# One VectorE step order for a two-layer attention block: weight splits, modulation sums and a turn moved to other places

## The chip, the cores and the metric

The kernel runs on one core of a Trainium2 chip. The metric is the device time of one execution in microseconds (us). It is taken as the median of several runs. A core has a matmul engine (TensorE, PE in the profile), a vector engine (VectorE, DVE), a scalar engine (ScalarE, ACT), GpSimd (POOL), and a queue that issues transfers (SyncE, SP). Each takes its instructions strictly in the order in which they are written, and they wait for one another on semaphores.

## The reference

The program computes two blocks. The change touches the first one only: two layers on 256 tokens of 1024 features, each with its own modulation.

```
cs = jax.nn.silu(c)
for l in range(DEPTH):                       # DEPTH = 2
    mod = cs @ w_ada[l] + b_ada[l]
    shift, scale, gate = mod[:, None, :D], mod[:, None, D:2 * D], mod[:, None, 2 * D:]
    h = rmsnorm(x, g_pre[l]) * (1.0 + scale) + shift
    y = hybrid_mixer(h, w_in[l], w_out[l], pe_k[l], pe_v[l], w_ck1[l], w_ck2[l], w_cv1[l], w_cv2[l])
    x = x + gate * rmsnorm(y, g_post[l])
...
    u = h @ w_in                             # hybrid_mixer: all projections from one product
...
    logits = jnp.concatenate([s_sel.reshape(MOBA_HEADS, Q_CHUNK, KM * MOBA_BLOCK), s_own], axis=-1)
    p = jax.nn.softmax(logits, axis=-1).astype(v_own.dtype)
...
    y = jnp.concatenate([o_m * jax.nn.silu(zm), o_n * jax.nn.silu(zn)], axis=-1)
    return y @ w_out
```

The mixer holds three kinds of attention (moba, selected and windowed) and one over compressed keys. The second block (neighbourhood attention, feed-forward, latent attention, eight experts) takes most of the time and is unchanged.

## The kernel before

**Two kinds of steps on one stream.** All weights come from memory as pieces of 128x2048 numbers (1 MB). SP issues them into a ring of six buffers `raw` (L681), in the order of the list `STEPS`. A piece is one of two kinds.

- `("w", n)`: a weight of a projection. A float32 product is made as three products of a high and a low part (`mm3`, L833 to L835), so the piece is split: ScalarE copies the rounded high part (`hi_to`, w_hi, L1625), then VectorE subtracts it (`raw_to`, w_lo, L2211). The splits live in a ring of three, so split n waits until TensorE has used split n-3. Below, w9 is the split of piece 9.
- `("ada", j, half)`: half of the modulation's part j. VectorE multiplies its four columns of 512 by the conditioning and adds them up in `acc` (four instructions, L2227 and L2229, in `raw_to` too). TensorE then sums over partitions with a product with ones (`ada`, L903 and L908), in bank 3, and ScalarE copies the result out (`ada_out`). Below, a3.1 is the second half of part 3. Parts 0 to 3 are shift and scale, 4 and 5 the gate.

A `raw` buffer is free when VectorE has done the step. Phase `pre` holds the first layer's parts 0 to 3. Phase `lay0` is the first layer and holds its parts 4 and 5 and parts 0 to 5 of the second layer. Phase `lay1` is the second layer and holds parts 0 to 5 of the next block's modulation.

**The start.** VectorE makes the eight halves of `pre`, with the norm of x (`normed`) after four of them. After the last, PE sums part 3, ScalarE copies it, VectorE makes scale and shift (`make_ab`), and then h, the normalised and modulated input, is made in four blocks: ScalarE and VectorE scale them, ScalarE makes the high parts (`h_hi`), and VectorE the low ones (`norm`, `lo(b)`). The first projection needs half of h and split 0 for its first half, and the rest of h and split 1 for its second. ScalarE copies out parts 1 to 3 and then makes the high parts of splits 0 to 2 (`hi_to(SPL)`), ahead of `h_hi`.

**The ticks.** After three projections comes a loop of 25 ticks (`LAY_TICKS`) over 24 pairs of heads. In tick i TensorE makes the scores of pair i+1, one or more pieces of the projections that are left (`fill`, table `LAY_FILL`), the turn (transpose) of the probabilities of pair i, further pieces, and the product of the values of pair i-1 (`values`; of a group's first pair in the next tick, and only when `finish` has emptied the output bank). VectorE makes the logits of pair i+1 (L2530), the finishing of a group of four pairs (`finish`), single operations of the compressed branch (`cmp_u` in tick 0 to `cmp_y` in tick 7), and at the tick's end the steps of `STEPS` up to a mark that `lay_steps_before` gives. ScalarE makes the exponentials of pair i+1 (L1880), copies the turned probabilities (L1894), empties the banks of a finished projection (`slot`), copies a modulation part (`ada_out`), and last makes the high part of the next split. A split's low part on VectorE so waits for a high part that comes last in ScalarE's tick, after the exponentials of that same tick's logits.

**The sums in the ticks.** `LAY_ADA` says in which tick TensorE sums which part: {1: 0, 4: 1, 9: 2, 10: 3, 12: 4, 15: 5}, always after the tick's scores and ahead of its projection pieces. In tick 1 it waits ahead of that for `cmp_u` and in tick 4 for `clogits`, since bank 3 is shared with the compressed branch. In tick 18 TensorE turns a part of y for the output projection (`turn_y`, L1014), which waits for `finish(3)`.

The order of VectorE's steps by tick of the first layer, before:

```
before the ticks  w0 w1 w2 | a4.0 w3 a4.1 w4 (of this layer) | a5.0 w5 a5.1 w6 | a0.0 w7 a0.1 w8 (of the next)
tick 2: a1.0 a1.1 w9     tick 4: a2.0 w10     tick 6: a2.1 a3.0 w11     tick 8: a3.1 w12
tick 9: a4.0 w13         tick 11: a4.1 a5.0 w14     tick 13: a5.1 w15
tick 15: w16     tick 16: w17     tick 18: w18     tick 22: w19
```

## Time and profile before

| | us |
|---|---|
| median of 3 runs (lowest to highest) | 1642.2 (1639.86 to 1644.54) |
| the profiled execution, device time | 1639.46 |
| its span in the trace | 1637.6 |
| PE busy, share of the span | 1412.2 (86%) |
| DVE busy, share of the span | 1215.8 (74%) |
| ACT busy, share of the span | 860.8 (53%) |
| first layer, from the start to its last product | 245.8 |
| second layer, to its last product | 453.9 |

The profiled execution stands 2.7 us under the median, and its span 1.9 us under its own device time. The two layers are the first 28% of the span. Times in the rows are in us from the span's start. A number in square brackets at a row's end is how long the engine was idle ahead of it, and who released it.

### The profile page before, as it was taken

How to read it: one execution, taken by the hardware profiler on the slowest of the kernel's cores; microseconds unless marked ns; L12 is line 12 of the kernel's file. 1: busy time of each engine (PE TensorE's matmuls, PEld its weight loads, DVE VectorE, ACT ScalarE, POOL GpSimd, SP SyncE). 2: the span in 40 equal slices, each digit the busy share in tenths (PEclk: the TensorE clock that was granted, in tenths of full speed). 3: DMA queues.
4: the chain of work that ended last, by engine and by line, in shares of the span. 5: the costliest groups of instructions: out<-in, count | busy, mean ns of one | idle time of the engine just before them, and what ended most of it. 6: DMA issues, size and time to landing. Idle time of an engine off the chain costs nothing.

```text
span 1637.6 us, 21240 instructions
## 1 busy us (share of the span) xinstructions
PE 1412.2 (86%) x7628; PEld 1185.4 (72%) x7628; DVE 1215.8 (74%) x1484; ACT 860.8 (53%) x1210; POOL 65.3 (4%) x82
## 2 busy tenths in 40 slices
PE   2799987899879996899985896999999999999992
PEld 2778777787668776898974875877777777777772
DVE  6777646776575747788857545789889888899895
ACT  2333534445443543343324635577677777777772
POOL 1000000000010000000001004000000000000001
PEclk8899998989988997999987996999999999999996
DMA  9765514545256623677763214899999999899782
GB/s 399 274 235 181 211 72 172 227 180 206 77 215 236 242 96 127 262 289 272 290 236 122 104 52 146 302 345 357 351 345 360 345 348 373 338 358 362 286 365 90
DMA packets 61537, 403.08 MB, mean 246 GB/s; under 512 B 6534, under 2 KB 9734, under 8 KB 15116
## 3 DMA queue, kind: packets, MB, share of 16 engines
q1 hardware_dynamic: 52416, 379.45, 61.2%
q10 hardware_dynamic: 7020, 15.17, 2.6%
q0 software_dynamic: 2016, 7.34, 1.2%
q8 instruction: 52, 0.85, 0.2%
q14 instruction: 33, 0.27, 0.0%
HBM read 393.01 MB, written 8.91 MB: 245 GB/s over the span
## 4 chain that ended last, share of the span: by engine, by line
PE 49%; DVE 32%; ACT 10%; issue 5%; DMA 2%; POOL 1%; ACTq 0%; DVEq 0%; SPq 0%; POOLq 0%
DVE w_lo L2211 18%; PE PS L833 13%; PE PS L835 12%; PE PS L834 12%; ACT w_hi L1625 4%; DVE acc L2229 4%; ACT xg L1720 2%; PE PS L903 1%; PE PS L986 1%; PE PS L1006 1%; DVE a_lo L2378 1%; DVE hb L2387 1%; DVE hb L2389 1%; DVE h_lo L2344 1%; PE PS L995 1%
## 5 line engine op out<-in xcount | busy, mean ns | idle before, releaser
L2211 DVE TENSOR_TENSOR w_lo<-raw,w_hi 128x2048 fp32r<-128x2048 f32 x287 | 659.4, 2298 | 156.4 <-ACT w_hi L1625 133.7
L1625 ACT ACTIVATE w_hi<-raw 128x2048 fp32r<-128x2048 f32 x287 | 547.7, 1919 | 243.3 <-PE PS L835 230.3
L833 PE MATMUL PS<-w_hi,h_hi 128*128 128x512 f32 (+2 forms) x812 | 335.3, 413 | 25.0 <-DVE h_lo L2654 7.3
L835 PE MATMUL PS<-w_hi,h_lo 128*128 128x512 f32 (+2 forms) x812 | 318.8, 393 | 0.0
L834 PE MATMUL PS<-w_lo,h_hi 128*128 128x512 f32 (+2 forms) x812 | 318.1, 392 | 0.0
L833 PE MATMUL PS<-h_hi,w_hi 128*128 128x256 f32 x776 | 235.2, 303 | 43.4 <-DVE w_lo L2211 19.4
L834 PE MATMUL PS<-h_lo,w_hi 128*128 128x256 f32 x776 | 227.4, 293 | 0.0
L835 PE MATMUL PS<-h_hi,w_lo 128*128 128x256 f32 x776 | 227.2, 293 | 0.0
L833 PEld LDWEIGHTS PS<-w_hi,h_hi 128*128 128x128 f32 x812 | 155.8, 192 | 72.8 <-DVE w_lo L2211 14.9
L2229 DVE SCALAR_TENSOR_TENSOR acc<-raw,cs,acc 128x512 f32<-128x512 f32 x252 | 189.5, 752 | 9.0
L833 PEld LDWEIGHTS PS<-h_hi,w_hi 128*128 128x128 f32 x776 | 156.9, 202 | 48.4 <-DVE w_lo L2211 19.6
L835 PEld LDWEIGHTS PS<-w_hi,h_lo 128*128 128x128 f32 x812 | 155.4, 191 | 32.8
L834 PEld LDWEIGHTS PS<-w_lo,h_hi 128*128 128x128 f32 x812 | 155.8, 192 | 28.6 <-issue 2.2
L834 PEld LDWEIGHTS PS<-h_lo,w_hi 128*128 128x128 f32 x776 | 156.8, 202 | 2.4 <-issue 1.7
L835 PEld LDWEIGHTS PS<-h_hi,w_lo 128*128 128x128 f32 x776 | 156.5, 202 | 0.0
L833 PE MATMUL PS<-w_hi,a_hi 128*128 128x512 f32 x340 | 140.2, 412 | 17.1 <-DVE a_lo L2378 11.1
L835 PE MATMUL PS<-w_hi,a_lo 128*128 128x512 f32 x340 | 134.5, 396 | 0.0
L834 PE MATMUL PS<-w_lo,a_hi 128*128 128x512 f32 x340 | 133.7, 393 | 0.0
L1880 ACT ACTIVATE lgp<-lgp,st 128x128 f32<-128x128 f32 (+1 forms) x96 | 42.9, 448 | 121.1 <-DVE st L2530 121.1
L833 PEld LDWEIGHTS PS<-w_hi,a_hi 128*128 128x128 f32 x340 | 64.6, 190 | 37.3 <-DVE w_lo L2211 22.9
L835 PEld LDWEIGHTS PS<-w_hi,a_lo 128*128 128x128 f32 x340 | 64.4, 189 | 14.7
L834 PEld LDWEIGHTS PS<-w_lo,a_hi 128*128 128x128 f32 x340 | 64.6, 190 | 11.9
(310 smaller groups left out, 1394.5 us busy)
## 6 DMA issues: line engine op xcount, KB each, us to landing
raw<-in_ws SPq DMA_DIRECT2D x359, 1024.0 KB, 5.6
y_rows<-ysb ACTq DMA_DIRECT2D x10, 512.0 KB, 7.6
rp<-in_rp ACTq DMA_DIRECT2D x8, 384.0 KB, 4.7
ckb<-in_ck ACTq DMA_DIRECT2D x2, 1024.0 KB, 4.8
y_rows<-ones ACTq DMA_DIRECT2D x3, 512.0 KB, 8.5
x<-in_x SPq DMA_DIRECT2D x1, 1024.0 KB, 13.4
gpost<-in_gpost ACTq DMA_DIRECT2D x2, 512.0 KB, 6.0
x_rows<-xn_f ACTq DMA_DIRECT2D x2, 512.0 KB, 3.9
```

Source lines behind the costliest of these rows:

```text
L833: t.matmul(out, lhs[0], rhs[0], start=start, stop=False, skip_group_check=True)
L834: t.matmul(out, lhs[0], rhs[1], start=False, stop=False, skip_group_check=True)
L835: return t.matmul(out, lhs[1], rhs[0], start=False, stop=stop, skip_group_check=True)
L903: last = t.matmul(PS[:, 3, c:c + 1], a[:, c * P:(c + 1) * P], ones[:, 0:1], start=True, stop=True)
L986: t.matmul(PS[:, PS_S[i % 2], 0:2 * u["nk"]].rearrange("p (a k) -> p a k", a=2), u["q"], u["k"], start=True, stop=True).then_inc(*e.inc("s ...
L995: last = t.transpose(PS[:, PS_PT, c * P:(c + 1) * P], lgp[:, i % 3, c * P:(c + 1) * P], ident)
L1006: last = t.matmul(PS[:, PS_O, h * HD:(h + 1) * HD], ptp[:, i % 2, (a * n + c) * P:(a * n + c + 1) * P], u["v"][a][c], start=c == 0, stop=c ...
L1625: a.activation(wh[:, SPL_AT[e.phase][i], :], raw[:, r, :], ACT.Copy).then_inc(*e.inc("hi"))
L1720: ins = a.activation(xg[:, kt, :], PS[:, 6 + kt // 4, (kt % 4) * P:(kt % 4 + 1) * P], ACT.Identity, scale=ab[:, 0, kt:kt + 1], bias=ab[:, ...
L1880: a.activation(part, part, ACT.Exp, bias=mn(c), scale=-1.0, accum_out=sm(c)).then_inc(*e.inc("probs"))
L2211: v.tensor_tensor(wl[:, s, :], raw[:, r, :], wh[:, s, :].bitcast(F32), ALU.subtract).then_inc(*e.inc("raw_used"))
L2229: ins = v.scalar_tensor_tensor(out=dst, in0=w, scalar=c[:, kt:kt + 1], in1=dst, op0=ALU.mult, op1=ALU.add)
```

## The change

It changes the order of work in the first block and no computation.

- **Start.** ScalarE makes the high part of split 0 between the copies of parts 1 and 2, and that of split 1 between those of parts 2 and 3. Split 2 comes after `h_hi`. VectorE does five halves ahead of `normed` in place of four, and the low part of split 0 ahead of `make_ab`.
- **Steps.** `layer_steps` gives a new order of the stream, w7 and w8 ahead of the sums, and VectorE goes through it by a table, `LAY_STEP`, one or two steps a tick up to tick 14. The second half of part 0 moves from ahead of the ticks into tick 0.
- **Sums.** On TensorE part 3 moves from tick 10 to 11 and part 4 from tick 12 to 13. Parts 0 and 1 (ticks 1 and 4) move to the end of their tick, with the waits for `cmp_u` and `clogits`, and so does the turn of y in tick 18.
- **Last split.** w19 moves from tick 22 to tick 23 on VectorE.

```
before the ticks  w0 | w1 w2 a4.0 w3 a4.1 w4 (of this layer) | a5.0 w5 a5.1 w6 w7 w8 | a0.0 (of the next)
tick 0: a0.1     tick 1: a1.0     tick 2: w9 a1.1     tick 4: w10     tick 5: a2.0     tick 6: w11     tick 7: a2.1
tick 8: w12 a3.0     tick 9: w13     tick 10: a3.1     tick 11: w14 a4.0     tick 12: a4.1 a5.0
tick 13: w15     tick 14: a5.1     tick 15: w16     tick 16: w17     tick 18: w18     tick 23: w19
```

The diff, cut to its core:

```
-LAY_ADA = {1: 0, 4: 1, 9: 2, 10: 3, 12: 4, 15: 5}
+LAY_ADA = {1: 0, 4: 1, 9: 2, 11: 3, 13: 4, 15: 5}
+
+LAY_STEP = [("ada", 0, 1), ("ada", 1, 0), ("ada", 1, 1), ("ada", 1, 1), ("w", 10), ("ada", 2, 0), ("w", 11), ("ada", 2, 1),
...
@@ tensor, in the ticks
-                    if i == 1:
-                        pe.wait_ge(*e.at("cmp_u", 1))
-                    if i == 4:
-                        pe.wait_ge(*e.at("clogits", 1))
-                    if i in LAY_ADA:
+                    if i in LAY_ADA and i > 4:
                         ada(unit + LAY_ADA[i])
-                    if i == 18:
-                        pe.wait_ge(*e.at("y", 2))
-                        bank_free(1)
-                        turn_y(1, 1, 1)
...
                         values(i - 1)
+                    if i in (1, 4):
+
+                        pe.wait_ge(*e.at("cmp_u" if i == 1 else "clogits", 1))
+                        ada(unit + LAY_ADA[i])
+                    if i == 18:
+                        pe.wait_ge(*e.at("y", 2))
+                        bank_free(1)
+                        turn_y(1, 1, 1)
@@ scalar, start
-            for j in range(1, 4):
-                ada_out(j, 1)
+            ada_out(1, 1)
             e.resume("lay0")
-            hi_to(SPL)
+            hi_to(1)
+            e.resume("pre")
+            ada_out(2, 1)
+            e.resume("lay0")
+            hi_to(2)
+            e.resume("pre")
+            ada_out(3, 1)
+            e.resume("lay0")
@@ vector
-            raw_to(4)
+            raw_to(5)
...
-                    split_to(1)
+                split_to(1)
...
-                split_to(9)
+                raw_to(step_of("ada", 0, 0))
...
-                    split_to(lay_steps_before(i) + SPL)
+                    if i < len(LAY_STEP):
+                        raw_to(step_of(*LAY_STEP[i]))
+                    else:
+                        split_to(min(lay_steps_before(i) + SPL, 19 if i < 23 else 20))
```

ScalarE at the start. L1680 copies a modulation part out in the kernel before (L1683 in the one after), L1625 (L1628) makes a high part, L1654 and L1658 (L1657 and L1661) are blocks of h. Before:

```order
L1680 ACTIVATE modc<-PS 128x4 x3
L1625 ACTIVATE w_hi<-raw 128x2048 x3
L1654 ACTIVATE hb<-PS,ab 128x256 x2
L1658 ACTIVATE h_hi<-hb 128x512 x2
L1651 DMA ckb<-in_ck 128x2048
```

After:

```order
L1683 ACTIVATE modc<-PS 128x4
L1628 ACTIVATE w_hi<-raw 128x2048
L1683 ACTIVATE modc<-PS 128x4
L1628 ACTIVATE w_hi<-raw 128x2048
L1683 ACTIVATE modc<-PS 128x4
L1657 ACTIVATE hb<-PS,ab 128x256 x2
L1661 ACTIVATE h_hi<-hb 128x512 x2
```

Two of the three high parts stand between the copies, and nothing stands between the last copy and the first block of h.

VectorE at the start, from the norm of x on (L2251 before, L2260 after). Before:

```order
L2251 TENSOR_SCALAR xn_l<-x,st 128x1024 x2
L2227 TENSOR_SCALAR acc<-raw,cs 128x512
L2229 SCALAR_TENSOR_TENSOR acc<-raw,cs,acc 128x512 x7
L2227 TENSOR_SCALAR acc<-raw,cs 128x512
L2229 SCALAR_TENSOR_TENSOR acc<-raw,cs,acc 128x512 x7
L2288 TENSOR_TENSOR modc<-modc,par 128x16
L2290 SCALAR_TENSOR_TENSOR ab<-modc,par 128x8
L2294 COPY ab<-modc 128x8
L2270 TENSOR_SCALAR hb<-PS,ab 128x256 x2
L2262 TENSOR_TENSOR h_lo<-hb,h_hi 128x512
L2270 TENSOR_SCALAR hb<-PS,ab 128x256 x2
L2262 TENSOR_TENSOR h_lo<-hb,h_hi 128x512 x3
```

After:

```order
L2260 TENSOR_SCALAR xn_l<-x,st 128x1024 x2
L2238 SCALAR_TENSOR_TENSOR acc<-raw,cs,acc 128x512 x4
L2236 TENSOR_SCALAR acc<-raw,cs 128x512
L2238 SCALAR_TENSOR_TENSOR acc<-raw,cs,acc 128x512 x7
L2220 TENSOR_TENSOR w_lo<-raw,w_hi 128x2048
L2297 TENSOR_TENSOR modc<-modc,par 128x16
L2299 SCALAR_TENSOR_TENSOR ab<-modc,par 128x8
L2303 COPY ab<-modc 128x8
L2279 TENSOR_SCALAR hb<-PS,ab 128x256 x2
L2271 TENSOR_TENSOR h_lo<-hb,h_hi 128x512
L2279 TENSOR_SCALAR hb<-PS,ab 128x256 x2
L2271 TENSOR_TENSOR h_lo<-hb,h_hi 128x512 x3
```

One half of a sum has gone ahead of the norm, and the low part of split 0 ahead of `make_ab`.

VectorE in ticks 6 and 7 of the first layer. The first y is the end of `cmp_y(0)` in tick 6, and lgp and st are logits. Before:

```order
L2609 TENSOR_TENSOR y<-y,tmpo 128x512
L2229 SCALAR_TENSOR_TENSOR acc<-raw,cs,acc 128x512 x4
L2227 TENSOR_SCALAR acc<-raw,cs 128x512
L2229 SCALAR_TENSOR_TENSOR acc<-raw,cs,acc 128x512 x3
L2211 TENSOR_TENSOR w_lo<-raw,w_hi 128x2048
L2530 ISA lgp,st<-lc,PS 128x128
```

After:

```order
L2622 TENSOR_TENSOR y<-y,tmpo 128x512
L2220 TENSOR_TENSOR w_lo<-raw,w_hi 128x2048
L2543 ISA lgp,st<-lc,PS 128x128
L2543 ISA st 128x1
L2543 ISA lgp,st<-lc,PS 128x128
L2543 ISA st 128x1
L2612 RECIPROCAL st<-st 128x8
L2613 TENSOR_TENSOR st<-st,vsw 128x8
L2617 TENSOR_TENSOR y<-PS,st 128x512
L2238 SCALAR_TENSOR_TENSOR acc<-raw,cs,acc 128x512 x4
```

Tick 6 has lost two halves of sums and keeps w11 alone, which now has nothing of the stream ahead of it. One of the halves stands in tick 7, the other in tick 8.

TensorE at the change from tick 10 to 11 of the first layer. L986 (L989) are scores, L903 (L906) the sum of part 3, and L1006 (L1009) values. Before, from the scores of tick 10 on:

```order
L835 MATMUL PS<-h_hi,w_lo 128x256
L986 MATMUL PS<-kswz,qn 128x256
L903 MATMUL PS<-ones,acc 128x1 x4
L1006 MATMUL PS<-vsw,ptp 128x64 x2
L833 MATMUL PS<-h_hi,w_hi 128x256
```

After, from the values at the end of tick 10 on:

```order
L838 MATMUL PS<-h_hi,w_lo 128x256
L1009 MATMUL PS<-vsw,ptp 128x64 x2
L989 MATMUL PS<-kswz,qn 128x512
L906 MATMUL PS<-ones,acc 128x1 x4
L836 MATMUL PS<-w_hi,h_hi 128x512
```

The sum of part 3 now stands behind the scores of tick 11, ahead of that tick's projection pieces.

## Rows read from the trace of the kernel before

**Rows 1.** The page's chain that ended last, by engine, as shares of the span.

```profile
PE 49%; DVE 32%; ACT 10%; issue 5%; DMA 2%; POOL 1%; ACTq 0%; DVEq 0%; SPq 0%; POOLq 0%
```

**Rows 2.** Stretches, both layers' ticks: length, busy PE, PEld, DVE, ACT, POOL, clock, DMA.

```profile
94.53:210.43 115.90, 107.14 (x614) 87.00 (x612) 84.64 (x180) 53.28 (x135) 0.00 (x0) 0.94 0.50 187
301.32:416.97 115.65, 103.98 (x609) 86.14 (x609) 83.37 (x179) 53.30 (x135) 0.00 (x0) 0.96 0.50 187
```

**Rows 3.** Timeline of PE at the start: start, duration, instruction, idle before.

```profile
33.79 1.87 PE L903 MATMUL PS<-ones,acc 128*128 128x1 f32 x8 [4.98 <-DVE acc L2229]
51.70 0.58 PE L833 MATMUL PS<-h_hi,w_hi 128*128 128x256 f32 x1 [16.05 <-DVE w_lo L2211]
```

**Rows 4.** Timeline of ACT at the start.

```profile
35.76 5.50 ACT L1625 ACTIVATE w_hi<-raw 128x2048 fp32r<-128x2048 f32 x3
41.16 1.01 ACT L1654 ACTIVATE hb<-PS,ab 128x256 f32<-128x256 f32 x2
```

**Rows 5.** Timeline of DVE at the start.

```profile
35.97 0.18 DVE L2288 TENSOR_TENSOR modc<-modc,par 128x16 f32<-128x16 f32 x1 [2.23 <-ACT modc L1680]
...
49.36 6.95 DVE L2211 TENSOR_TENSOR w_lo<-raw,w_hi 128x2048 fp32r<-128x2048 f32 x3
```

**Rows 6.** Line L681, the issues of pieces 0 and 1, with time to landing.

```profile
L681 SPq DMA_DIRECT2D raw<-in_ws x1: 328/328/328, 15.6 to 15.6; - x1
...
DMA to landing us min/median/max: 15.8/15.8/15.8
...
L681 SPq DMA_DIRECT2D raw<-in_ws x1: 327/327/327, 18.7 to 18.7; - x1
...
DMA to landing us min/median/max: 15.1/15.1/15.1
```

**Rows 7.** DVE groups by line, first layer's ticks: count, busy, mean ns, idle before.

```profile
L2229 DVE SCALAR_TENSOR_TENSOR acc<-raw,cs,acc 128x512 f32<-128x512 f32 x35 | 26.3, 752 | 1.2
L2211 DVE TENSOR_TENSOR w_lo<-raw,w_hi 128x2048 fp32r<-128x2048 f32 x11 | 25.2, 2292 | 18.3 <-ACT w_hi L1625 18.1
```

**Rows 8.** Timeline of DVE in the ticks of the first layer.

```profile
94.53 0.29 DVE L2530 CUSTOM_DVE_ANT_0 lgp<-lc,PS 128x128 f32<-128x128 f32 x1 [0.22 <-DVE vsw L2677]
...
196.81 0.29 DVE L2530 CUSTOM_DVE_ANT_0 lgp<-lc,PS 128x128 f32<-128x128 f32 x1 [0.23 <-DVE w_lo L2211]
...
200.19 2.29 DVE L2211 TENSOR_TENSOR w_lo<-raw,w_hi 128x2048 fp32r<-128x2048 f32 x1 [2.76 <-ACT w_hi L1625]
```

**Rows 9.** Timeline of ACT in tick 15 of the first layer.

```profile
191.29 0.60 ACT L1894 ACTIVATE ptp<-PS 128x512 f32<-128x512 f32 x1 [0.25 <-PE PS L995]
191.79 0.59 ACT L1682 ACTIVATE gate<-PS 128x512 f32<-128x512 f32 x1
192.26 1.92 ACT L1625 ACTIVATE w_hi<-raw 128x2048 fp32r<-128x2048 f32 x1
```

**Rows 10.** Timeline of PE in the ticks of the first layer.

```profile
120.69 0.49 PE L903 MATMUL PS<-ones,acc 128*128 128x1 f32 x3 [2.55 <-DVE ce L2579]
...
149.02 0.58 PE L833 MATMUL PS<-h_hi,w_hi 128*128 128x256 f32 x1 [2.92 <-ACT qm L1829]
...
154.87 0.95 PE L903 MATMUL PS<-ones,acc 128*128 128x1 f32 x8
```

**Rows 11.** Stretches around two PE waits, with the granted clock (last but two).

```profile
145.20:148.60 3.40, 0.91 (x6) 0.50 (x5) 2.81 (x9) 1.72 (x7) 0.00 (x0) 1.00 0.90 354
148.60:152.00 3.40, 2.98 (x14) 2.98 (x15) 3.22 (x8) 1.85 (x8) 0.00 (x0) 0.50 0.65 270
...
206.60:210.00 3.40, 3.40 (x13) 2.13 (x11) 1.66 (x7) 2.05 (x7) 0.00 (x0) 0.51 0.02 10
```

**Rows 12.** Timelines of DVE and PE near the end of the first layer.

```profile
229.30 2.29 DVE L2211 TENSOR_TENSOR w_lo<-raw,w_hi 128x2048 fp32r<-128x2048 f32 x1 [4.61 <-ACT w_hi L1625]
...
232.37 0.50 PE L833 MATMUL PS<-w_hi,h_hi 128*128 128x512 f32 x1 [1.14 <-DVE h_lo L2654]
```

**Rows 13.** Timeline of ACT before the ticks of the second layer.

```profile
292.92 1.90 ACT L1625 ACTIVATE w_hi<-raw 128x2048 fp32r<-128x2048 f32 x1
```

More of the change, by code:

```diff
@@ L53 @@
 LAY_FILL = [(1, 2) if i % 4 == 3 and i < 16 else (1, 1) for i in range(18)] + [(0, 0)] * (LAY_TICKS - 18)
-LAY_ADA = {1: 0, 4: 1, 9: 2, 10: 3, 12: 4, 15: 5}
+LAY_ADA = {1: 0, 4: 1, 9: 2, 11: 3, 13: 4, 15: 5}
+LAY_STEP = [("ada", 0, 1), ("ada", 1, 0), ("ada", 1, 1), ("ada", 1, 1), ("w", 10), ("ada", 2, 0), ("w", 11), ("ada", 2, 1),
+            ("ada", 3, 0), ("w", 13), ("ada", 3, 1), ("ada", 4, 0), ("ada", 5, 0), ("w", 15), ("ada", 5, 1)]
 LAY_OUT = {19: 2, 20: 2, 21: 2, 22: 2}
@@ L98, in layer_steps @@
 def layer_steps(gates):
-    place = [(6, 0, 0), (7, 0, 1), (8, 1, 0), (8, 1, 1), (9, 2, 0), (10, 2, 1), (10, 3, 0), (11, 3, 1),
-             (12, 4, 0), (13, 4, 1), (13, 5, 0), (14, 5, 1)]
+    place = [(8, 0, 0), (8, 0, 1), (8, 1, 0), (9, 1, 1), (10, 2, 0), (11, 2, 1), (12, 3, 0), (13, 3, 1),
+             (14, 4, 0), (14, 4, 1), (14, 5, 0), (15, 5, 1)]
     out = []
@@ L2519, in layer, with step_of @@
                     gate_post()
+                def step_of(kind, n, half=None):
+                    step = ("w", n) if kind == "w" else ("ada", n + 6 * (l == 0), half)
+                    return STEPS[e.phase].index(step) + 1
                 def logits(i):
```

## The prediction

> **What bounds the kernel now.** I read the chain that ended last first, to see which engines hold the end. PE has half of it, and VectorE and ScalarE another 42% [rows 1], so no engine is bound by itself and hand-overs between the three count. Then I took the stretch from a layer's first logits to its output projection. It is 115.90 us in the first layer and 115.65 in the second, while PE is busy for 107.1 and 104.0 of it [rows 2]. PE could save at most 9 to 12 us a layer there. The timelines show where PE stands still. Before the first projection it waits 16.05 us, for the low part of split 0 [rows 3]. In the ticks it waits 2.55 us for the compressed branch's logits, ahead of the sum of part 1, and 2.92 us for a bank that ScalarE empties late [rows 10]. At the end of the layer there is a wait of 1.14 us [rows 12].
>
> **The start.** At 33.79 PE sums part 3, ScalarE copies it, and three high parts follow at 35.76, 5.50 us long, ahead of the first block of h at 41.16 [rows 3, 4]. Piece 0 lands at 15.6 + 15.8 = 31.4 us and piece 1 at 18.7 + 15.1 = 33.8 [rows 6]. So ScalarE can make the first high part at 31.4 to 33.3. Only then does it copy part 2 (33.5). PE needs bank 3 from that copy for part 3: 33.5 in place of 33.79. The second high part runs at 33.8 to 35.7, the copy of part 3 ends at 35.9, and `make_ab` starts at 36.0, as before at 35.97 [rows 5]. Nothing is gained up to here, and the norm that VectorE makes one half later is hidden. The first block of h then starts at 36.6 in place of 41.16: 4.6 us. PE's first product needed, after half of h at 45.4, two more low parts of h and the low part of split 0 at 49.36 to 51.7 [rows 5]. That low part is now there first, so PE starts at about 40.9 in place of 51.70: **10.8 us**. The later splits follow. The low part of split 1 ends at 47.2 and PE asks for it at 49.3. After that each split costs VectorE 2.29 and half a sum about 2.9 [rows 7], under PE's 5.8 a split. Piece 4 is issued when split 0 is done, 16 us sooner. Ahead of the ticks a0.1 (3.1 us) is gone, but w8 now waits for a high part that had been hidden behind it. Of the 3.1 us some 0.5 are left: the first logits start at **83.2 in place of 94.53, 11.3 us earlier**. The second layer has no such start. There its high part 8 runs from 292.92 [rows 13], its low part ends at 297.2 and a0.0 at 300.1, so the first logits come 0.9 us earlier.
>
> **The ticks.** Durations: a low part 2.32 with its gap, a first half of a sum 2.86, a second half 3.14 (4 x 0.752 and gaps) [rows 7]. A pair of logits takes 0.86 or 1.1. The hand-over decides. From the start of a pair's logits it takes two exponentials, the copy of the turned probabilities and a high part until the low part can start: 200.19 - 196.81 = 3.38 us [rows 8], and 3.97 for the wide pairs. Before, in all seven such ticks up to tick 13, VectorE made one or two halves of sums first and hid all or part of that time. Now the low part comes first, and the half behind it. I walked VectorE through the new table from 83.2, each low part at the later of VectorE's own end and ScalarE's high part:
>
> - tick 0 with a0.1 ends at 90.0, tick 1 with a1.0 at 95.2.
> - tick 2: logits 95.4, w9 at 98.8, VectorE idle 2.75. Tick 3: the compressed logits end at 111.5.
> - tick 4: w10 at 115.9 (idle 2.2). PE sums part 1 at 111.6 at once.
> - tick 6: w11 at 128.1 (1.1). Tick 8: w12 at 139.2 (2.7). Tick 9: w13 at 148.1 (0.9). Tick 10: a3.1 ends at 154.5.
>
> Up to there PE is ahead. At tick 8 it is at 133.8 where it was at 149.02 [rows 10], 15 us earlier. But then it runs into the moved sums. The sum of part 3 stands ahead of tick 11's pieces and turn, and PE reaches it at 152 and waits until 154.5. Behind it stand the turn of pair 11, the copy on ScalarE, the high part 14 and the low part 14: 0.8 + 1.5 + 0.5 + 0.4 + 2.0 later, at 159.8, and VectorE idles 4 us from 155.6. The same ring comes twice more. a4.1 ends at 169.3 and PE, there at 166.4, starts the sum of part 4. w15 starts at 176.9, a5.1 ends at 183.5, PE is there at 180.7. After that sum (2.0), a piece (1.5) and the turn, ScalarE copies, copies the gate and starts the high part 16 0.97 after its copy [rows 9]. VectorE starts w16 at 190.6 and w17 at 196.55, which ends at 198.85. Before, w17 ended at 202.5 [rows 8]. From the first logits on that is 115.65 against 107.95 us, so **the ticks cost 7.7 us more in the first layer**, and by the same walk 7.95 in the second, whose stretch was 0.25 us shorter before [rows 2]. Of the 7.7, 3.1 are a0.1, which moved in, and the rest low parts that wait in the open. PE's 2.55, 2.92 and later waits do vanish. They are replaced by four of 2.5 to 4 us in ticks 10, 11, 13 and 15, the first of them ahead of the values of pair 8, for VectorE's `finish(1)`.
>
> **The end of a layer.** The low part 19 holds VectorE until 231.6, after a wait of 4.61, and the low part of y behind it lets PE start at 232.37 [rows 12]. With w19 behind it, that low part starts 1.05 us earlier, and w19 is still ready 0.6 us before PE needs it: **1.05 us less in each layer**. The turn of y in tick 18 moves nothing. What PE needs next is a low part in tick 19 that the logits of tick 18 lead to.
>
> **The clock.** After PE stood for 2.9 us the next 3.4 us had the granted clock at 0.50, the 1.2 GHz level, and so had a stretch after the wait at 203 [rows 11]. At half the clock PE's work takes up to twice as long. The new waits in ticks 11, 13 and 15 are as long, and what runs behind them (sum, piece, turn) is on the ring. Each such stretch can cost up to 1.6 us: 0 to 4.8 a layer. I take 2.3, half, since part of a stretch falls on work that has room: **4.6 us**, bounds 0 and 9.6.
>
> The Trainium skill, "TensorE: Matmul & The Clock Gate", section "Why this matters for your kernels", sets the limit for a harmless gap in PE's work somewhat above these lengths. By it the term would be 0. This trace does not agree, since it shows the drop behind 2.92 us.
>
> **The sum.** -11.3 (start) + 7.7 - 1.05 (first layer) - 0.9 + 7.95 - 1.05 (second) + 4.6 (clock) = +6.0 us, rounded. On the profiled execution's 1639.5 that is 1645.5. It stood 2.7 under the median, so the median goes from 1642.2 to **1648.2**.
>
> **The rivals.**
>
> 1. The ring doesn't cost clock. Everything else as above: +1.4, 1643.6. For it: a stretch at the low clock that starts late falls on pieces ahead of the next wait, and then only shortens that wait. Chance 0.30.
> 2. **Faster.** The ticks keep their length, because the sums find their halves ready and ScalarE's high parts come soon enough: -11.3 - 0.9 - 2.1 = -14.3, 1628. For it: PE is 15 us ahead at tick 8 and has no wait of its own left. Against it: VectorE's own work from tick 8 to 15 with its open waits is longer than PE's. It decides whether a3.1 ends before PE stands at the sum of part 3, for which VectorE must be 2.5 us sooner. Chance 0.17.
> 3. The start brings little: ScalarE is in order, so if pieces 0 and 1 land late, the copies of parts 2 and 3 and so h wait for them. Each us of delay costs one, all of it gone would be 1648.2 + 11 = 1659. The landings in the rows speak against it, with 0.1 us of room. Chance 0.06, and as much again for what I don't see.
>
> My forecast has 0.41. The range goes from 1634 (rival 1 with the ticks 10 us cheaper in all by my reading of hand-overs) to 1657 (all of the clock term and 4 more). A change of 0.3%, 4.9 us, is about what a measurement of this kernel can tell from none. Slower by more than that is most of the forecast and of rival 3 and a little of rival 1: 0.46. Within it: 0.34. Faster: 0.20.
>
> **What would show it.** In the trace after: the first product at 41 and the first logits near 83 (the start). VectorE idle ahead of each low part in ticks 2, 8 and 11, by 2.7, 2.7 and 4 us. PE waiting for acc at the sums of ticks 11, 13 and 15, some 3 us each, and no wait for the bank in tick 8. From first logits to output projection about 123.6 us and more, against 115.9. The granted clock at 0.50 behind the new waits. I am wrong if that stretch stays under 118 in both layers, or if the first product starts after 45.

## The result and the profile after

The changed kernel takes 1649.8 us (median of 6 runs, 1648.5 to 1654.2) against 1642.4 us (median of 6, 1639.9 to 1644.5). The ratio is 1.0054, 95% interval 1.0038 to 1.0069. It is **7.5 us slower**, where 6.0 was forecast.

The profiled execution of after was the longest of its six, 1654.2 us with a span of 1652.4, and the one of before was short for its kernel (1639.5, span 1637.6). So the two traces stand 14.8 us apart, twice the medians. What follows reads places and sizes from the traces, and the worth of an edit from the medians.

The stretches of both layers' ticks, from the first logits to the output projection, answer to [rows 2], in the same columns:

```profile
84.14:214.54 130.40, 112.73 (x616) 89.73 (x615) 87.70 (x184) 53.30 (x135) 0.00 (x0) 0.91 0.47 172
305.28:433.14 127.86, 111.06 (x609) 88.78 (x608) 86.42 (x183) 53.15 (x135) 0.00 (x0) 0.91 0.49 176
```

With the boundaries on PE (the transposes that open the second layer start at 254.57 before and 259.31 after, those of the phase behind it at 462.69 and 477.81), the difference of the traces lies here:

| stretch | before | after | difference |
|---|---|---|---|
| start to first logits | 94.53 | 84.14 | -10.4 |
| ticks, first layer | 115.90 | 130.40 | +14.5 |
| end of the first layer | 44.14 | 44.77 | +0.6 |
| second layer to its logits | 46.75 | 45.97 | -0.8 |
| ticks, second layer | 115.65 | 127.86 | +12.2 |
| end of the second layer | 45.72 | 44.67 | -1.05 |
| all behind the layers | 1174.9 | 1174.6 | -0.3 |

The start first. The timeline of PE there (start, duration, instruction, idle before), against [rows 3]:

```profile
33.74 1.84 PE L906 MATMUL PS<-ones,acc 128*128 128x1 f32 x8 [5.72 <-ACT modc L1683]
41.42 0.55 PE L836 MATMUL PS<-h_hi,w_hi 128*128 128x256 f32 x1 [5.84 <-DVE h_lo L2271]
```

PE's wait ahead of the first product has fallen from 16.05 us to 5.84. It ends with h, since the low part of split 0 had been ready since 35.9. The other wait, ahead of the sum of part 3, was there before too (4.98 us, for VectorE). It is now 5.72, for ScalarE's copy of part 2, and the sum starts at nearly the same time (33.74, was 33.79).

In the ticks, VectorE's low parts wait. The timeline of VectorE in the first layer, ticks 2, 8, 11, 13, 15 and 16:

```profile
99.73 2.29 DVE L2220 TENSOR_TENSOR w_lo<-raw,w_hi 128x2048 fp32r<-128x2048 f32 x1 [2.75 <-ACT w_hi L1628]
...
140.30 2.29 DVE L2220 TENSOR_TENSOR w_lo<-raw,w_hi 128x2048 fp32r<-128x2048 f32 x1 [3.16 <-ACT w_hi L1628]
...
162.01 2.29 DVE L2220 TENSOR_TENSOR w_lo<-raw,w_hi 128x2048 fp32r<-128x2048 f32 x1 [5.46 <-ACT w_hi L1628]
...
182.32 2.29 DVE L2220 TENSOR_TENSOR w_lo<-raw,w_hi 128x2048 fp32r<-128x2048 f32 x1 [4.18 <-ACT w_hi L1628]
...
198.17 2.29 DVE L2220 TENSOR_TENSOR w_lo<-raw,w_hi 128x2048 fp32r<-128x2048 f32 x1 [8.43 <-ACT w_hi L1628]
...
204.30 2.29 DVE L2220 TENSOR_TENSOR w_lo<-raw,w_hi 128x2048 fp32r<-128x2048 f32 x1 [2.99 <-ACT w_hi L1628]
```

All low parts of this stretch together (line L2220: what VectorE sat idle for, us, times; the same question to before gave 12.4 us, 4 times):

```profile
  ACT w_hi L1628: 30.3, 9
```

And PE waits for VectorE's halves of sums, `acc` in the table of waits of PE for the same stretch (who waited for whom: us in total, times, longest; the line with `h_lo` is the wait that ends the stretch):

```profile
PE PS L911 <- DVE acc L2238: 4.5, 2, 3.1
PE PS L836 <- DVE h_lo L2667: 2.9, 1, 2.9
PE PS L906 <- DVE acc L2238: 2.8, 1, 2.8
```

The place where both meet is tick 11. PE reaches the sum of part 3 too early and stands for 2.78 us. The turn of pair 11 follows only at 158.99, on it ScalarE's copy at 159.66, its high part at 159.99 and VectorE's low part at 162.01:

```profile
155.49 1.05 PE L906 MATMUL PS<-ones,acc 128*128 128x1 f32 x8 [2.78 <-DVE acc L2238]
158.99 0.63 PE L998 MATMUL PS<-par,lgp 128*128 128x128 f32 x2
...
171.51 2.08 PE L911 MATMUL PS<-acc,ones 128*128 128x512 f32 x2 [3.11 <-DVE acc L2238]
173.52 2.07 PE L913 MATMUL PS<-brow,ones 1*128 1x512 f32 x2
175.52 0.80 PE L836 MATMUL PS<-w_hi,h_hi 128*128 128x512 f32 x1
...
178.25 1.05 PE L998 MATMUL PS<-par,lgp 128*128 128x128 f32 x4
```

```profile
159.66 0.38 ACT L1903 ACTIVATE ptp<-PS 128x256 f32<-128x256 f32 x1 [2.44 <-PE PS L998]
159.94 0.17 ACT L1683 ACTIVATE modc<-PS 128x4 f32<-128x4 f32 x1
159.99 1.92 ACT L1628 ACTIVATE w_hi<-raw 128x2048 fp32r<-128x2048 f32 x1
```

The sum of part 5 waits 1.39 us. At all three sums the granted clock falls to its lower level: from 156.5 to 159.9 behind the first, and at the other two as here (columns: window, length, busy PE, clock, DMA share, GB/s; compare [rows 11]):

```profile
166.80:170.20 3.40, 1.60 (x8) 1.00 0.99 361
170.20:180.40 10.20, 8.89 (x18) 0.50 0.68 255
180.40:190.60 10.20, 8.81 (x44) 1.00 0.34 113
190.60:197.40 6.80, 6.80 (x18) 0.51 0.34 142
```

In the ticks the clock stood at 1.2 GHz for 23.8 us in the first layer, where it had been 13.6 before, and for 24.0 in the second, where it had been 10.2.

What that did to the work is seen at the sum of part 4. In the lines above, the sum and the piece behind it take 4.01 and 2.73 us. In the kernel before, at 2.4 GHz, the same two took 2.00 and 1.52:

```profile
171.00 1.02 PE L908 MATMUL PS<-acc,ones 128*128 128x512 f32 x2
...
173.00 0.50 PE L833 MATMUL PS<-w_hi,h_hi 128*128 128x512 f32 x1
...
174.52 0.60 PE L995 MATMUL PS<-par,lgp 128*128 128x128 f32 x4
```

### The profile page after: what moved, and what is told of

Same layout as the page of the kernel before. It is cut to its first block, busy times and chain, and to the rows that moved or that the text cites. A ratio compares the mean times of both kernels' runs of the same rounds, so it can differ in the third digit from the quotient of the medians.

```text
span 1652.4 us, 21240 instructions
## 1 busy us (share of the span) xinstructions
PE 1425.1 (86%) x7628; PEld 1191.9 (72%) x7628; DVE 1216.2 (74%) x1484; ACT 861.0 (52%) x1210; POOL 65.5 (4%) x82
## 4 chain that ended last, share of the span: by engine, by line
PE 48%; DVE 33%; ACT 10%; issue 5%; DMA 3%; POOL 1%; ACTq 0%; DVEq 0%; SPq 0%; POOLq 0%
DVE w_lo L2220 17%; PE PS L836 13%; PE PS L838 12%; PE PS L837 12%; DVE acc L2238 5%; ACT w_hi L1628 4%; DMA raw<-in_ws 2%; ACT xg L1723 2%; DVE a_lo L2387 1%; DVE hb L2396 1%; DVE hb L2398 1%; DVE h_lo L2353 1%; PE PS L913 1%; PE PS L1009 1%; PE PS L911 1%
## 5 line engine op out<-in xcount | busy, mean ns | idle before, releaser
L2220 DVE TENSOR_TENSOR w_lo<-raw,w_hi 128x2048 fp32r<-128x2048 f32 x287 | 659.6, 2298 | 183.7 <-ACT w_hi L1628 161.3
L1628 ACT ACTIVATE w_hi<-raw 128x2048 fp32r<-128x2048 f32 x287 | 547.8, 1918 | 246.2 <-PE PS L838 222.2
L836 PE MATMUL PS<-w_hi,h_hi 128*128 128x512 f32 (+2 forms) x812 | 340.2, 419 | 26.7 <-DVE h_lo L2667 9.1
L837 PE MATMUL PS<-w_lo,h_hi 128*128 128x512 f32 (+2 forms) x812 | 321.9, 396 | 0.0
L836 PEld LDWEIGHTS PS<-w_hi,h_hi 128*128 128x128 f32 x812 | 158.6, 195 | 75.9 <-DVE w_lo L2220 14.8
L836 PE MATMUL PS<-w_hi,a_hi 128*128 128x512 f32 x340 | 140.3, 413 | 17.2 <-DVE a_lo L2387 11.2
L838 PEld LDWEIGHTS PS<-w_hi,a_lo 128*128 128x128 f32 x340 | 64.4, 190 | 14.7
L837 PEld LDWEIGHTS PS<-w_lo,a_hi 128*128 128x128 f32 x340 | 64.6, 190 | 11.8
```

The source lines that it names most:

```text
L836: t.matmul(out, lhs[0], rhs[0], start=start, stop=False, skip_group_check=True)
L837: t.matmul(out, lhs[0], rhs[1], start=False, stop=False, skip_group_check=True)
L838: return t.matmul(out, lhs[1], rhs[0], start=False, stop=stop, skip_group_check=True)
L1628: a.activation(wh[:, SPL_AT[e.phase][i], :], raw[:, r, :], ACT.Copy).then_inc(*e.inc("hi"))
L2220: v.tensor_tensor(wl[:, s, :], raw[:, r, :], wh[:, s, :].bitcast(F32), ALU.subtract).then_inc(*e.inc("raw_used"))
```

## Theory and rivals

The theory is the prediction's: the start gives some 11 us, and the new order of steps takes more than that back, through low parts of VectorE that wait in the open and through a **ring**: half of a sum on VectorE, the sum on PE, the turn behind it, ScalarE's copy and high part, VectorE's low part, and only then the next half. Rivals: the loss comes from the sums and the turn of y at a tick's end; from the clock behind PE's waits and not from the order; or the open low parts alone do it and no ring is closed. All ratios below are against the kernel before, timed on the same chip beside each experiment (1641.6, 1642.0 and 1642.1 us in the three groups), with the 95% interval.

## Experiments: the parts apart

**The start alone**, on the kernel before (in the first layer also `split_to(1)` ahead of `make_ab`):

```diff
-            for j in range(1, 4):
-                ada_out(j, 1)
...
-            hi_to(SPL)
+            ada_out(1, 1)
...
+            hi_to(1)
...
+            ada_out(2, 1)
...
+            hi_to(2)
...
+            ada_out(3, 1)
...
-            raw_to(4)
+            raw_to(5)
```

> The kernel before with the start of the change alone: the first high parts between the copies of parts 1, 2 and 3, raw_to(5), and the low part of split 0 ahead of make_ab in the first layer. If the start is worth what the sum says, first product at 41 and first logits 10.4 to 11.3 us earlier than 94.53 and nothing given back in the unchanged ticks: 1642.4 - 11 = 1631. Rival, the gain is lost again because VectorE has the same steps to do before PE needs them: 1638 to 1642, with new waits of PE in the ticks.

Measured: 1629.8 us, ratio 0.9927 (0.9908 to 0.9946), 11.8 us less. First product 41.29, first logits 84.58, ticks 114.9 and 115.7 us long, as before. The start is worth what the sum said, and the old order of steps gives nothing back.

**The new order of steps alone**, on the kernel before:

```diff
-    place = [(6, 0, 0), (7, 0, 1), ...
+    place = [(8, 0, 0), (8, 0, 1), ...
-LAY_ADA = {1: 0, 4: 1, 9: 2, 10: 3, 12: 4, 15: 5}
+LAY_ADA = {1: 0, 4: 1, 9: 2, 11: 3, 13: 4, 15: 5}
...
-                    split_to(lay_steps_before(i) + SPL)
+                    if i < len(LAY_STEP):
+                        raw_to(step_of(*LAY_STEP[i]))
+                    else:
+                        split_to(lay_steps_before(i) + SPL)
```

> The kernel before with the new order of steps alone (place, LAY_STEP, the sums of parts 3 and 4 one tick later, the step a0.0 as the last ahead of the ticks); sums 0 and 1, the turn of y and w19 stand where they stood, and the start is the old one. If the order of steps costs 7.7 and 7.95 us in the ticks, less 0.9, and the clock 4.6: 1642.4 + 19.4 = 1662. If the clock costs nothing: 1657. Rival, the loss of the change sits in the turn and the sums at a tick's end and not in the steps: 1645 or less.

Measured: 1674.6 us, ratio 1.0198 (1.0182 to 1.0215), **33 us more**. The loss is in the order of steps, and larger than forecast. The ticks are 135.8 and 132.9 us. Part of it is a pairing that the full change does not have: with the sums of parts 0 and 1 at a tick's start, PE stands ahead of them too, 3.10 us in tick 1 (3.36 in the second layer, where the trace names the half of part 0) and 3.98 in tick 4, for the compressed logits, where it had been 2.55 [rows 10].

**The ends alone**: sums 0 and 1 and the turn of y at a tick's end, and w19 in tick 23, on the kernel before:

```diff
-                    if i in LAY_ADA:
+                    if i in LAY_ADA and i > 4:
                         ada(unit + LAY_ADA[i])
...
                         values(i - 1)
+                    if i in (1, 4):
...
+                        ada(unit + LAY_ADA[i])
+                    if i == 18:
...
+                        turn_y(1, 1, 1)
```

> The kernel before with the sums of parts 0 and 1 and the turn of y in tick 18 at the tick's end on PE, and w19 in tick 23 in place of 22, nothing else. If PE's waits in tick 4 (2.55 and 3.0 us) are hidden by VectorE's chain, only w19 counts, 1.05 us a layer: 1642.4 - 2.1 = 1640.3. Rival, these waits are on the path and go: 5 us more, 1635.

Measured: 1635.7 us, ratio 0.9960 (0.9946 to 0.9973), 5.9 us less. The rival had 5 us more than the sum and seemed right, so w19 was tried by itself:

```diff
-                    split_to(lay_steps_before(i) + SPL)
+                    split_to(min(lay_steps_before(i) + SPL, 19 if i < 23 else 20))
```

> The kernel before with w19 in tick 23 in place of 22, nothing else. By the prediction 1.05 us a layer: 1642 - 2.1 = 1639.9, and so 3.8 of the 5.9 us of e4_ends belong to PE's sums and turn at the tick's end. Rival, w19 brings nothing and all 5.9 are theirs: 1642.

Measured: 1635.8 us, ratio 0.9967 (0.9953 to 0.9980), 6.3 us less. Both expectations fail: w19 alone brings all of it, and the sums and the turn at a tick's end nothing on the old order, as the prediction had it. The trace shows w19's own share: in the first layer PE's wait for that low part falls from 1.14 [rows 12] to 0.18 us and the last group of products of the layer starts 1.27 us sooner. The traces put 2.0 us more in the phase behind the layers (see the last section). The other 3 us are in no trace: the profiled execution of before was 2.7 us faster than its median, so its trace doesn't show what a usual one loses.

**All but the order of steps**: the changed kernel with the old tables, and `split_to` in every tick and ahead of the ticks.

```diff
-LAY_ADA = {1: 0, 4: 1, 9: 2, 11: 3, 13: 4, 15: 5}
+LAY_ADA = {1: 0, 4: 1, 9: 2, 10: 3, 12: 4, 15: 5}
...
-    place = [(8, 0, 0), (8, 0, 1), (8, 1, 0), (9, 1, 1), (10, 2, 0), (11, 2, 1), (12, 3, 0), (13, 3, 1),
+    place = [(6, 0, 0), (7, 0, 1), (8, 1, 0), (8, 1, 1), (9, 2, 0), (10, 2, 1), (10, 3, 0), (11, 3, 1),
```

> The changed kernel without its new order of steps: the start, the sums 0 and 1 and the turn of y at a tick's end and w19 in tick 23, on the old steps (places, halves per tick, sums of parts 3 and 4 in ticks 10 and 12). If the two gains measured apart add, 11.8 for the start and 5.9 for the ends: 1641.6 - 17.7 = 1624. Rival, they overlap because both only move PE ahead of VectorE: 1628 to 1630.

Measured: 1624.6 us, ratio 0.9898 (0.9880 to 0.9916), 17.4 us less; the two gains add. So the change is a gain of 17.4 us and an order of steps that costs **25.3** on top of it (1649.8 - 1624.6).

## Experiments: what in the order costs

**Halves ahead of the low part** in three ticks of the changed kernel:

```diff
-LAY_STEP = [("ada", 0, 1), ("ada", 1, 0), ("ada", 1, 1), ("ada", 1, 1), ("w", 10), ("ada", 2, 0), ("w", 11), ("ada", 2, 1),
-            ("ada", 3, 0), ("w", 13), ("ada", 3, 1), ("ada", 4, 0), ("ada", 5, 0), ("w", 15), ("ada", 5, 1)]
+LAY_STEP = [("ada", 0, 1), ("ada", 1, 0), ("w", 9), ("w", 9), ("w", 10), ("ada", 2, 0), ("w", 11), ("ada", 2, 1),
+            ("w", 12), ("w", 13), ("ada", 3, 1), ("w", 14), ("ada", 5, 0), ("w", 15), ("ada", 5, 1)]
...
-    place = [(8, 0, 0), (8, 0, 1), (8, 1, 0), (9, 1, 1), (10, 2, 0), (11, 2, 1), (12, 3, 0), (13, 3, 1),
-             (14, 4, 0), (14, 4, 1), (14, 5, 0), (15, 5, 1)]
+    place = [(8, 0, 0), (8, 0, 1), (8, 1, 0), (8, 1, 1), (10, 2, 0), (11, 2, 1), (11, 3, 0), (13, 3, 1),
+             (13, 4, 0), (14, 4, 1), (14, 5, 0), (15, 5, 1)]
```

> The changed kernel, with the order inside three ticks turned back: in ticks 2, 8 and 11 the half of a sum stands ahead of the low part (a1.1 w9, a3.0 w12, a4.0 w14), and the stream's order with it. If low parts that wait in the open are what the ticks cost, 2.75 + 3.2 + 5.5 us of VectorE's waits shrink by a half's 2.9 each, some 6 us a layer where they are on the path: 1649.8 - 10 = 1640. Rival, the moved sums of parts 3 to 5 set the length (a3.1, a4.1 and a5.1 end when they end, since the three ticks hold the same work): within 2 us of 1649.8.

Measured: 1634.3 us, ratio 0.9950 (0.9930 to 0.9970), 15.5 us less than the change, more than the 10 expected. The same steps in the same ticks, three neighbours exchanged. The low parts of ticks 2 and 8 no longer wait (19.3 us of waits in place of 30.3), and PE's wait for the sum of part 4 is gone. Those for parts 3 and 5 stay, 2.79 and 2.27 us. The ticks are 118.5 and 119.1 us.

**Only tick 11 of the three**:

```diff
-            ("ada", 3, 0), ("w", 13), ("ada", 3, 1), ("ada", 4, 0), ("ada", 5, 0), ("w", 15), ("ada", 5, 1)]
+            ("ada", 3, 0), ("w", 13), ("ada", 3, 1), ("w", 14), ("ada", 5, 0), ("w", 15), ("ada", 5, 1)]
...
-             (14, 4, 0), (14, 4, 1), (14, 5, 0), (15, 5, 1)]
+             (13, 4, 0), (14, 4, 1), (14, 5, 0), (15, 5, 1)]
```

> The changed kernel with the order turned back in tick 11 alone, a4.0 ahead of w14, of the three ticks that together brought 15.5 us. If the losses of the three ticks simply add by their open waits (2.75 in tick 2, 3.16 in tick 8, 5.46 in tick 11), tick 11 has almost half: 1642. If the ring through the moved sums makes tick 11 the one that counts, nearly all: 1636. Rival, tick 11's wait is only made by what is late before it: 1648.

Measured: 1637.3 us, ratio 0.9978 (0.9964 to 0.9992), 12.5 of the 15.5. Ticks 2 and 8, with more than half of the open waits of the three between them, are worth 3 by the medians. So an open wait of VectorE costs most where PE's next sum hangs on it, in tick 11. How little the other two cost is less sure: by the two traces they are worth 6.9 us in the stretches of the ticks and 3.2 to the end of the second layer.

**The sums at a tick's end.** The order of steps stays as in the change. PE sums parts 3, 4 and 5 behind the turn and the pieces of ticks 11, 13 and 15, and ScalarE copies each behind its high parts:

```diff
-                    if i in LAY_ADA and i > 4:
+                    if i == 9:
                         ada(unit + LAY_ADA[i])
...
+                    if i in (11, 13, 15):
+                        ada(unit + LAY_ADA[i])
...
-                    if i in LAY_ADA:
+                    if i in LAY_ADA and i < 11:
                         ada_out(unit + LAY_ADA[i], 1)
...
                     hi_to(lay_steps_before(i) + SPL)
+                    if i in LAY_ADA and i > 10:
+                        ada_out(unit + LAY_ADA[i], 1)
```

> The changed kernel with the sums of parts 3, 4 and 5 at the end of ticks 11, 13 and 15 on PE, and ScalarE's copy of each behind its high parts of the tick. If the ring through these sums (VectorE's half, sum, turn, high part, low part) makes the open waits of VectorE ahead of w14, w15 and w16 (5.46, 4.18 and 8.43 us), they shrink to what a low part first costs by itself, about 3 each, and PE's turns are not late: 3 to 4 us a layer and the clock term, 1641. Rival, the low part ahead of the half costs by itself and the ring adds nothing: within 2 us of 1649.8.

Measured: 1631.2 us, ratio 0.9935 (0.9918 to 0.9951), **18.6 us less** than the change, twice what was expected. All low parts still come first and still wait, but the waits of ticks 11, 13 and 15 are 3.0, 0.4 and 3.0 us and not 5.5, 4.2 and 8.4. The timeline of VectorE in this kernel:

```profile
158.20 2.29 DVE L2224 TENSOR_TENSOR w_lo<-raw,w_hi 128x2048 fp32r<-128x2048 f32 x1 [2.98 <-ACT w_hi L1630]
...
174.76 2.29 DVE L2224 TENSOR_TENSOR w_lo<-raw,w_hi 128x2048 fp32r<-128x2048 f32 x1 [0.43 <-ACT w_hi L1630]
...
185.15 2.29 DVE L2224 TENSOR_TENSOR w_lo<-raw,w_hi 128x2048 fp32r<-128x2048 f32 x1 [2.98 <-ACT w_hi L1630]
```

The ring is there, and the place of its sums is worth more than anything else tried alone. The rival, that the ring adds nothing, is refuted. That a low part ahead of a half costs nothing outside the ring is not shown; the run with both cures, below, speaks against it. Nor does this run part the order from the clock: at 1.2 GHz its ticks spend 13.4 and 13.7 us, 10.5 and 10.3 less than those of after, and from the durations above each of these is worth up to half its length.

**ScalarE's half of that edit alone** (its last two hunks, from `-                    if i in LAY_ADA:` on, with PE as in the change):

> The changed kernel with ScalarE's copies of the sums of parts 3, 4 and 5 behind its high parts of the tick, while PE's sums stay at the start of ticks 11, 13 and 15. If PE's place is what closes the ring (the turn stands behind the sum, ScalarE waits for the turn anyway, and its copy takes 0.17 us), the time stays: within 2 us of 1649.8. Rival, ScalarE's copy ahead of the high part is the link: towards 1631.

Measured: 1644.9 us, ratio 1.0023 (1.0010 to 1.0037), 4.9 of the 18.6. Outside the 2 us that were allowed, so the copies ahead of the high parts seem to have a part in it, but the place of PE's sum has the larger one, the other 13.7. Of the 4.9, the traces put 2.0 in the phase behind the layers (last section), so the copies' part is less sure than the number.

**Both cures together**, halves ahead of low parts and sums at a tick's end:

> The changed kernel with both cures, each of which was measured alone: a half of a sum ahead of the low part in ticks 2, 8 and 11 (1634.3) and the sums of parts 3 to 5 at the tick's end (1631.2). If low parts in the open and the ring are two costs, most of both comes: 1622 to 1625. Rival, both cures break the same ring, only at another place: 1630.

Measured: **1614.3 us**, ratio 0.9833 (0.9810 to 0.9856), 27.8 us less than before and 35.5 less than the change. The cures bring 15.5 and 18.6 apart, 34.1 in sum, so they add, and the time is below both that were expected. With the sums already at the tick's end the three exchanges still bring 16.9 us (1631.2 to 1614.3). So a low part ahead of a half costs outside the ring of the sums too. In the first layer PE's waits for `tmpo`, the end of a group in `finish`, fall from 5.8 us to 2.5 with them. The stretches of the ticks of this kernel are shorter than those of the kernel before, 115.90 and 115.65:

```profile
83.41:196.36 112.95, 105.76 (x616) 86.65 (x615) 87.70 (x184) 53.33 (x135) 0.00 (x0) 0.95 0.54 199
286.85:396.64 109.79, 101.11 (x609) 83.20 (x608) 86.41 (x183) 53.19 (x135) 0.00 (x0) 0.98 0.57 205
```

and the waits of PE in the first of them are down to these:

```profile
PE PS L836 <- DVE h_lo L2671: 2.9, 1, 2.9
PE PS L1009 <- DVE tmpo L2651: 2.5, 3, 1.5
PE PS L1009 <- DVE y L2647: 1.6, 1, 1.6
```

None is for a half of a sum, and VectorE's low parts wait 11.2 us in all.

**The same sums on the old order of steps**, with ScalarE's copies behind its high parts there too:

```diff
+                    if i in (10, 12, 15):
+                        ada(unit + LAY_ADA[i])
```

> The changed kernel on the old order of steps (as e5_rest, 1624.55), and the sums of parts 3, 4 and 5 at the end of ticks 10, 12 and 15 on PE with ScalarE's copies behind its high parts. If the ring through the sums exists in the old order too (w16 waited 5.28 us there, w12 1.97), 2 to 3 us a layer go: 1620. Rival, with the old order the halves are done before PE asks and the ring is not closed: within 1.5 us of 1624.5.

Measured: 1626.4 us, ratio 0.9903 (0.9882 to 0.9924), against 1624.6 and 0.9898 (0.9880 to 0.9916) without it. The two intervals all but coincide, and both have ticks of 114.8 and 116.6 or 116.7 us, so the 1.8 us between the medians are not told from none. On the old order there is no ring to open: the halves are done when PE asks. In the first layer of the kernel before none of the sums of parts 2 to 5 has a wait (the first of them is in [rows 10]). So the new order, with both cures, is 10.3 us better than the best that was measured with the old one (1624.6). Which of its moves brings that, no run shows; three neighbours and the place of three sums hid it.

**The clock.** Spare products on PE ahead of the waits of the sums of parts 3 and 4:

```diff
             def ada(j):
 
+                if e.phase in ("lay0", "lay1") and j - 6 * (e.phase == "lay0") in (3, 4):
+                    pe.wait_ge(*e.at("bank3", used[3]))
+                    for c in range(8):
+                        t.matmul(PS[:, 3, 0:P], ones[:], ones[:], start=True, stop=True)
```

> The changed kernel with eight spare products of 128x128 by 128x128 on PE ahead of the wait of the sums of parts 3 and 4 in each layer, which work on constants and write to the bank that the sum overwrites. The waits of 2.78 and 3.11 us in the first layer would become work of about 1.7 and a wait of 1.1 to 1.4. If the fall of the clock behind these waits costs time: no stretch at 0.50 behind them, and 1649.8 - 3 to 6, 1645. Rival, the clock falls on work that has room: within 1.5 us of 1649.8.

Measured: 1650.2 us (1645.1 to 1650.7), ratio 1.0055 (1.0039 to 1.0072): no gain. In the first layer of its trace the spare products took 1.95 us and covered the wait of the sum of part 3 wholly (2.78 us in after), and no lower clock stands behind it. The sum of part 4 still waits 1.51 us, the sum of part 5, which has none, 1.57, and behind each of these short waits the clock fell. PE, and the windows around (columns as above):

```profile
168.47 1.13 PE L915 MATMUL PS<-acc,ones 128*128 128x512 f32 x2 [1.51 <-DVE acc L2242]
...
183.52 1.12 PE L915 MATMUL PS<-acc,ones 128*128 128x512 f32 x2 [1.57 <-DVE acc L2242]
```

```profile
171.00:174.40 3.40, 3.40 (x12) 0.52 0.98 386
...
184.60:188.00 3.40, 3.40 (x7) 0.53 0.75 299
188.00:191.40 3.40, 3.40 (x12) 0.50 0.00 0
```

The expectation was that no such stretch would be left, and that failed, so the run does not tell what the clock costs. Its profiled execution, with ticks of 126.5 and 124.1 us, was the shortest of its six and that of after the longest, so the two traces do not tell it either. What it costs in the median stays open; what it cost in the profiled execution of after is read below.

The runs in one table. Ticks are the stretches of both layers in the profiled execution:

| kernel | us | ticks |
|---|---|---|
| before | 1642.4 | 115.9, 115.7 |
| after | 1649.8 | 130.4, 127.9 |
| start alone | 1629.8 | 114.9, 115.7 |
| order alone | 1674.6 | 135.8, 132.9 |
| ends and w19 alone | 1635.7 | 115.1, 116.7 |
| w19 alone | 1635.8 | 115.7, 116.8 |
| after without the order | 1624.6 | 114.8, 116.6 |
| the same, sums at the end | 1626.4 | 114.8, 116.7 |
| after, three ticks turned back | 1634.3 | 118.5, 119.1 |
| after, tick 11 turned back | 1637.3 | 122.8, 121.7 |
| after, sums at the end | 1631.2 | 119.2, 119.2 |
| after, ScalarE's copies late | 1644.9 | 124.8, 126.2 |
| after, spare products | 1650.2 | 126.5, 124.1 |
| both cures | 1614.3 | 113.0, 109.8 |

## Why the prediction was right, and where it was not

**The start** (-11.3). Right: 10.3 us for the first product (41.42, forecast 40.9) and 10.4 for the logits in the trace, 11.8 in the run of the start alone. The half microsecond short is h, which began at 36.80 in place of 36.6.

**The walk through the ticks** (+7.7, +7.95). Counted from the first logits, in us:

| | w9 | w10 | w11 | w12 | w13 | a3.1 ends | w14 | w15 | w16 | w17 ends |
|---|---|---|---|---|---|---|---|---|---|---|
| forecast | 15.6 | 32.7 | 44.9 | 56.0 | 64.9 | 71.3 | 76.6 | 93.7 | 107.4 | 115.7 |
| after | 15.6 | 32.4 | 44.5 | 56.2 | 65.0 | 71.3 | 77.9 | 98.2 | 114.0 | 122.5 |
| with spare products | 15.6 | 32.4 | 44.4 | 55.5 | 64.4 | 70.7 | 76.1 | 94.1 | 110.3 | 118.5 |

Up to the half that closes the ring the walk holds within 0.6 us. From there the trace of after falls behind by 6.8 us to the end of w17, in the ticks with the long stretches at 1.2 GHz. The execution with the spare products, which had no stretch over 6.8 us there, falls behind by 2.9. So the ring was at the place and nearly of the size forecast, and what was **mis-sized is the clock term**: 2.3 us a layer were taken; the trace of after has 6.8 (14.5 - 7.7) and 4.3 (12.2 - 7.95). The parts of the ring that PE does account for most of this. A sum and the piece behind it, in us:

| | part 3 | part 4 | part 5 |
|---|---|---|---|
| at 2.4 GHz (part 3 in the second layer of after, 4 and 5 in before) | 0.9 + 1.5 | 2.0 + 1.5 | 2.0 + 1.5 |
| after, first layer | 0.9 + 2.6 | 4.0 + 2.7 | 2.4 + 2.7 |
| after, second layer | 0.9 + 1.5 | 4.0 + 2.7 | 2.6 + 2.7 |

That is some 6 us lost in the first layer and 5 in the second, near the 6.8 and 4.3. Where the clock did not fall, at the sum of part 3 in the second layer, VectorE's wait in tick 11 was 4.09 us, as forecast (4), and not 5.46. The term took stretches of 3.4 us at the lower level; those at parts 4 and 5 were 10.2 and 6.8 long, in both layers. The 11.1 us of this execution lie outside the bounds of 0 to 9.6. It was 4.4 us over its median. If all of that was in the ticks, which is an estimate, some 7 us are in a usual run, against 4.6.

Two of the waits forecast came out otherwise. Those of PE at the sums were to be some 3 us each; they are 2.78, 3.11 and 1.39 in the first layer, 1.26, 3.33 and 1.63 in the second. And the wait for the compressed logits ahead of the sum of part 1 did not vanish: 1.71 of its 2.55 us stayed.

**w19** (-1.05 a layer). The traces agree: 0.96 us of wait gone, the end of the second layer 1.05 us shorter. The two runs with it gained more, 5.9 and 6.3 us, for reasons outside the layers.

**The sums and the turn at a tick's end** (nothing). Right on the old order: with and without them 1635.7 and 1635.8.

**The second layer's earlier logits** (-0.9): 0.8.

**The sum** came out 1.5 us too small, and two errors in it go against each other. By the medians, the order of steps costs 25.3 us where the terms for it (7.7 + 7.95 - 0.9 + 4.6) gave 19.4, and the ends with w19 bring 5.9 where 2.1 stood. The start brings 0.5 more. The first two differences, +5.9 and -3.8, have a common part that was not forecast at all, the length of the phase behind the layers, told in the last section: 2.8 us of the first and 3.0 of the second by the traces. That they nearly cancel is luck, and the 1648.2 is better than its terms.

**The harmless gap.** The Trainium skill, "TensorE: Matmul & The Clock Gate", section "Why this matters for your kernels", calls gaps in PE's work harmless up to a limit that waits of 1.5 us are far below. The runs do not agree: the low level stands behind waits of 1.51 and 1.57 us.

**The rivals.** The faster one fell for this kernel but named the condition well. It said that the ticks keep their length if a3.1 is ready when PE stands at the sum of part 3. Both cures give this, and the ticks are then 113.0 and 109.8. Its price, -14.3, was too small: the kernel with them is at -27.8. That the start brings little had nothing for it. That the ring costs no clock is not settled by the run meant for it, but in the trace of after it is wrong by the 6 and 5 us above.

## What to carry to other kernels

Follow a wait through all engines until it comes back to the one that waits: an instruction that PE takes ahead of the transposes of a tick closes a ring if VectorE's input to it stands behind a step that needs those transposes. Put such an instruction behind what feeds the other engines, and on an in-order engine put independent work ahead of a step that waits; each was worth 15 to 19 us here, and they added. And undo the parts of a change one by one: a change that lost 7.5 us held 17.4 of gain outright, and 10.3 more with six places exchanged.

## What the runs showed of the hardware

**The length of a wait alone did not tell where the clock fell.** In after, a wait of PE of 2.49 us ended at 147.6, and the clock stayed at 1.00 until 156.5, behind the next wait; one of 1.98 us ended at 121.2, with the lower level from 122.4. In the run with spare products, 1.51 us were enough.

**A stretch at the lower clock can be three times as long behind the same wait, in a phase that nobody touched.** In the phase behind the layers PE waits 3.30 us for a low part at 517.90 in the kernel before and at 518.22 in the one with the ends. Its profile rows (window, length, busy PE, clock, DMA share, GB/s) are, before:

```profile
462.70:631.70 169.00, 148.85 (x872) 0.91 0.50 189
517.10:520.50 3.40, 2.60 (x12) 0.52 0.96 400
520.50:527.30 6.80, 6.80 (x28) 0.50 0.97 387
```

and with the ends:

```profile
463.00:629.00 166.00, 145.95 (x872) 0.93 0.51 192
517.50:520.90 3.40, 2.68 (x12) 0.57 0.92 381
520.90:527.70 6.80, 6.80 (x53) 0.97 0.99 392
```

Same work, same wait, and 10.2 us at 1.2 GHz against 3.4: the phase takes 169.0 us or 166.0. After has the long form (168.9), and so have the start alone (169.1) and tick 11 turned back (168.8). The kernels with both cures, with the sums at the end, with spare products, with the order alone and without the order have the short one (166.0 to 166.2). Three lie between: three ticks turned back and ScalarE's copies late (both 166.8) and w19 alone (167.1). So the phase makes up 2 to 3 of the 4 us that w19 and the ends gained beyond their own 2, and 2.8 of the 25.3. Whether an edit upstream sets it, through the moment at which the phase begins, or whether it changes from one execution to the next, is open: there is one trace of each kernel, and the runs of the kernel before lie between 1635.4 and 1645.9 us. A gain of under 3 us in this kernel should therefore be read in the trace, at its place, before it is believed.
